# Carrying the last transposes of a sub-layer into the next one, in a two-layer hybrid decoder on eight cores

## What is computed

```python
for i in range(DEPTH):
    h = rms_norm(x, norm_g[i, 0])
    if i % N_MIXERS == 0:
        m, vr = spatial_gate_mixer(h, sg_w_in[j], sg_ln_g[j], sg_ln_b[j], sg_w_s[j], sg_b_s[j], sg_w_out[j])
    else:
        m, S = gla_mixer(h, gla_w_in[j], ..., gla_w_out[j], gla_init[j])
    x = x + rms_norm(m, norm_g[i, 1])
    h = rms_norm(x, norm_g[i, 2])
    x = x + rms_norm(swiglu(h, ffn_w13[i], ffn_w2[i]), norm_g[i, 3])
```

## Time and profile before

| | us |
|---|---|
| median of 2 runs | 2412.22 (2394.37 and 2430.08) |
| profiled execution | 2396.78 |
| its span, slowest core (6) | 2395.2 |
| spans of the eight cores | 2367.0 to 2395.2 |
| PE, DVE, ACT, POOL busy | 1819.7, 683.4, 693.8, 377.5 |
| TensorE's granted clock, mean of core 6 | 0.880 |

### The profile page before, as it was taken

One profiled execution on the slowest core, in us unless ns is written; L12 is line 12 of the kernel. 1 busy time (PEld: TensorE's weight loads), 2 busy tenths in 40 slices (PEclk: granted clock), 3 DMA queues, 4 the chain that ended last, 5 costly groups with the idle time before them and its releaser, 6 DMA issues.

```text
span 2395.2 us, 28534 instructions; the slowest of 8 cores (2367.0 to 2395.2 us)
## 1 busy us (share of the span) xinstructions
PE 1819.7 (76%) x9813; PEld 867.2 (36%) x9813; DVE 683.4 (29%) x1509; ACT 693.8 (29%) x1280; POOL 377.5 (16%) x447
## 2 busy tenths in 40 slices
PE   1698967697688966698587967599558898764698
PEld 0344423343344433343234433244224443321353
DVE  1422123312332122322233122322253212234222
ACT  2332134311422135411422125411423213542211
POOL 2011111311101111411111110411111111030010
PEclk9899988798799988699789988799779899875799
DMA  9789967289597959089696959189754882916572
GB/s 140 97 119 128 145 98 114 36 121 161 98 140 112 152 85 136 9 127 150 128 141 91 164 76 136 18 124 143 172 104 67 132 132 36 159 27 210 128 114 61
DMA packets 267997, 271.37 MB, mean 113 GB/s; under 512 B 17808, under 2 KB 261152, under 8 KB 267456
## 3 DMA queue, kind: packets, MB, share of 16 engines
q0 software_dynamic: 233088, 222.46, 64.6%
q1 hardware_dynamic: 26320, 38.71, 5.9%
q10 hardware_dynamic: 8448, 8.39, 1.1%
HBM read 473.44 MB, written 18.55 MB: 205 GB/s over the span
## 4 chain that ended last, share of the span: by engine, by line
PE 61%; DVE 11%; DMA 8%; ACT 7%; issue 7%; POOL 4%; SPq 1%; DVEq 0%; ACTq 0%; POOLq 0%
PE ps L244 57%; DMA yp<-t 4%; ACT t L313 2%; POOL t L303 2%; DVE t L602 2%; ACT t L331 1%; PE pt L348 1%; DMA t<-st_in 1%; DMA t<-sg_ln_b 1%; DVE t L369 1%; POOL t L942 1%; DVE t L372 1%; DVE t L388 1%; SPq L295 1%; DVE t L392 1%
## 5 line engine op out<-in xcount | busy, mean ns | idle before, releaser
L244 PE MATMUL ps<-t,t 128*128 128x512 bf16 (+4 forms) x8312 | 1656.6, 361 | 75.2 <-DVE t L923 25.4
L244 PEld LDWEIGHTS ps<-t,t 128*128 128x128 bf16 (+1 forms) x8312 | 750.7, 101 | 948.8 <-issue 217.2
L1054 DVE TENSOR_TENSOR t<-t,ps 128x512 bf16<-128x512 bf16 (+3 forms) x244 | 128.6, 541 | 510.5 <-PE ps L244 492.3
L348 PE MATMUL pt<-t,t 128*128 128x128 bf16 (+1 forms) x544 | 52.0, 255 | 286.6 <-ACT t L331 216.9
L262 POOL DMA_DIRECT2D t<-ffn_w x144 | 125.8, 876 | 895.9 <-PE ps L244 823.6
L1052 ACT ACTIVATE t<-ps 128x512 bf16<-128x512 f32 (+3 forms) x244 | 117.1, 480 | 502.5 <-PE ps L244 496.9
L303 POOL TENSOR_TENSOR t<-t,t 128x1 f32<-128x1 f32 (+1 forms) x136 | 74.8, 550 | 568.2 <-DVE t L301 568.2
L348 PEld LDWEIGHTS pt<-t,t 128*128 128x128 bf16 (+1 forms) x544 | 40.6, 115 | 306.6 <-issue 304.9
L313 ACT ACTIVATE t<-t 128x1024 bf16<-128x1024 f32 (+1 forms) x68 | 71.7, 1054 | 230.3 <-DVE t L372 103.2
L353 DVE TENSOR_TENSOR t<-pt,t 128x1024 bf16<-128x1024 bf16 (+1 forms) x68 | 79.0, 1169 | 141.9 <-PE pt L348 141.8
L301 DVE TENSOR_SCALAR t<-t 128x1 f32<-128x1 f32 (+1 forms) x136 | 20.5, 151 | 295.4 <-ACT t L313 165.4
(11 more groups left out here) (126 smaller groups left out, 1055.0 us busy)
## 6 DMA issues: line engine op xcount, KB each, us to landing
t<-ffn_w POOLq DMA_DIRECT2D x112, 1024.0 KB, 14.5
t<-sg_w_in POOLq DMA_DIRECT2D x32, 1024.0 KB, 20.1
t<-gla_w_in POOLq DMA_DIRECT2D x24, 1024.0 KB, 14.7
t<-sg_w_out POOLq DMA_DIRECT2D x16, 1024.0 KB, 19.9
t<-ffn_w POOLq DMA_DIRECT2D x16, 768.0 KB, 12.2
t<-xp SPq DMA_DIRECT2D x16, 512.0 KB, 5.1
t<-norm_g SPq DMA_DIRECT2D x16, 512.0 KB, 6.7
t<-ffn_w POOLq DMA_DIRECT2D x16, 512.0 KB, 9.5
```

The lines of the kernel that those rows point to most:

```text
L244: ins = e.matmul(out_ap, l, r, start=(i == 0), stop=(i == n - 1))
L348: ins = e.transpose(pt[:, pb, kc * 128: kc * 128 + np_], hbuf[0:np_, kc * 128:(kc + 1) * 128], ident[0:np_, 0:np_])
L1054: P.op(DVE, lambda e: e.tensor_tensor(out=gTf[:, j, t0:t1], in0=sab[sb][:, 0:n], in1=bank(ba + 1, 128, n), op=ALU.mult), reads=[("sab", sb ...
```

## The change

A list `carryB` holds `norm_in_B` calls that are put off, and `pop_carry` makes them: with a tile as argument the first one if it is that tile's, without one all of them. It is used at four places in passes 0 to 2:

- end of the gMLP mixer and end of the GLA mixer: `norm_in_B` of tile 3 is carried and made in the FFN behind its three units on tiles 0 to 2, ahead of the deferred units;
- end of FFN 0: the lag becomes 2, and `norm_in_B` of the last tile is carried and made in the V projection, ahead of tile 3's matmuls;
- end of FFN 1: `norm_in_A` of tiles 0 to 3 stays, and `norm_in_B` of all four is carried into the next mixer, each ahead of its tile's `vA`.

`hbx` gets addresses of its own at the end of SBUF, since it is now read while the mixer's tiles are in use.

```diff
+    HBX0 = (229344 - 4 * 2048) // 64 * 64
...
-    hbx = [alloc([128, D], BF16, a) for _ in range(4)]
+    assert a[0] <= HBX0
+    a_hbx = [HBX0]
+    hbx = [alloc([128, D], BF16, a_hbx) for _ in range(4)]
...
+    carryB = []
+
+    def pop_carry(tile=None):
+        while carryB and (tile is None or carryB[0][0] == tile):
+            norm_in_B(*carryB.pop(0))
+            if tile is not None:
+                break
...
                 for (t, np_) in tiles:
+                    pop_carry(t)
                     vA(t, np_)
...
-                norm_in_B(*pend)
+                if last:
+                    norm_in_B(*pend)
+                else:
+                    carryB.append(pend)
...
                         for (t, np_) in tiles:
+                            pop_carry(t)
                             b = bcx[0] % 4
...
-                        norm_in_B(te, 128, stt_[te]["hi"], li * 2 + 1)
+                        if (not last) and te == ptl[-1]:
+                            carryB.append((te, 128, stt_[te]["hi"], li * 2 + 1))
+                        else:
+                            norm_in_B(te, 128, stt_[te]["hi"], li * 2 + 1)
...
                     if jj == 0 and ci == NSPLIT - 1:
+                        pop_carry()
                         for d_ in deferred:
                             ab_unit(*d_)
...
-                lagn = (len(tiles) + 1) if final else 1
+                lagn = (len(tiles) + 1) if final else (2 if split else 1)
...
             while pendq:
-                norm_in_B(*pendq.pop(0))
+                if (not last) and len(pendq) == 1:
+                    carryB.append(pendq.pop(0))
+                else:
+                    norm_in_B(*pendq.pop(0))
             for (t, np_) in chained:
                 hi = norm_in_A(t, np_, xi=t)
-                pendq.append((t, np_, hi, 0))
-            while pendq:
-                norm_in_B(*pendq.pop(0))
+                carryB.append((t, np_, hi, 0))
```

More of the change, by code:

```diff
@@ L188, in _build @@
     mixs = alloc([16, 2048], BF16, a)
+    assert a[0] <= HBX0, (a[0], HBX0)
     a = phase_alloc()
```

## The result

| | before | after |
|---|---|---|
| median, us | 2398.09 (10 runs, 2391.72 to 2430.08) | 2463.78 (11 runs, 2441.08 to 2666.99) |
| ratio, 95% interval | | 1.0215 [1.0179, 1.0251] |
| profiled execution, us | 2396.78 | 2464.41 |
| span of the slowest core (6) | 2395.2 | 2462.8 |
| median span of cores 0 to 3 | 2378.8 | 2431.5 |

The ratio leaves out disturbed runs, in which the cores of one die showed a lower clock, and the medians don't; in the profiled execution after, too, cores 4 to 7 hold stretches of 66 to 162 us at a clock of 0.81 and cores 0 to 3 none, so what follows is read on core 0, or as a median over cores, unless it says core 6. 1.0215 on 2396.8 us is +51.5 us; the interval leaves no doubt that the kernel is slower, but it doesn't settle whether by more than 2%. A second series gave 1.022 [1.0168, 1.0272].

What follows compares the result with a forecast made beforehand. The prediction took TensorE's work plus its idle stretches, which also lower its clock, as the bound. Terms -9 (A), -22.5 (B), 0 (C) and +82.2 (D) sum to +50.7 on 2396.8 us: 2447, range 2428 to 2479.

Steps and rivals of the forecast that it cites:

- A: End of gMLP mixer to FFN 0: tile 3's transposes behind three units shorten TensorE's gap; -9 us over three passes.
- B: FFN 0 to GLA: lag of 2 and V projections ahead of tile 3's transposes; -22.5 us over three passes.
- C: GLA to FFN 1: 1.5 us gained at unit 0, 1.6 us waited in the deferred units; sum 0.
- D: FFN 1 to next pass's mixer: copies queue behind statistics on VectorE, TensorE idles; +82.2 us over three boundaries.
- The rival in which VectorE takes a ready copy first: At the pass boundary, ready copies pass the statistics, so deferral gains there: 2341 us, faster by 2.3%; chance 0.06.
- The holes: Idle TensorE ahead of `vA(1)`, `vA(2)` and `vA(3)` at each pass boundary: 7.6, 7.6 and 6.0, together 21.2 us.
- The earlier start: Next mixer's `vA(0)` starts at 613.6 instead of 615.41, at the low clock; worth 1.0 us a boundary.
- The low clock: Matmuls restarting after each of three pass-boundary gaps run at 0.50: 2.4 us a gap, 7.2 in all.
- The rows I named beforehand: Profile after: transposes' wait for ScalarE falls some 60 us; new matmul-for-copy row, nine waits of 6 to 8 us.
- Late slabs: Gains at FFN 0 and GLA don't arrive because weight slabs come late: 2479 us; chance 0.08.
- Bursts that never come back to the full clock: Pass boundary: each 32-matmul burst takes 13.8 us, never reaching full clock; +40, 2488 us; chance 0.05.
- A clock that doesn't fall: In the pass-boundary gaps the clock stays up: 20 us less, 2427 us; chance 0.05.

Runs made afterwards that it cites:

- the interleaved kernel: The changed kernel with norm_in_B of tiles 0 and 1 written between the norm_in_A, those of tiles 2 and 3 ahead of the statistics: 2353.59 us, 0.9807.
- the kernel without D: The changed kernel with the four norm_in_B at the pass boundary made ahead of the mixer again, everything else kept: 2370.14 us, 0.9878.

## Why the prediction was right

It gave 2447 us for a run like the profiled one, +50.7. The ratio gives +51.5; the measured median, 2463.78, lies in the range (2428 to 2479) 17 us above the figure. The narrower range of the forecast, 2434 to 2462, isn't the sum of its terms' bounds, which is 2427 to 2468; +51.5 lies inside either. By place, after against before in the stretches above:

| | predicted | measured |
|---|---|---|
| A | -9 | -6.9 |
| B | -22.5 | -22.6 |
| C | 0 | +0.3 |
| D | +82.2 | +74.6, and +2.9 up to the u projection |
| sum | +50.7 | +48.3 |

The remaining 3 us up to the ratio's 51.5 are in none of the four stretches; where they are is open. The mechanisms and the terms came out as forecast, to a few us; that the sum is within 1 us is luck, since D was put 4.7 us too high, A 2.1 us too good, and 3 us have no place.

**What TensorE waits for.** The step that decided the case was to ask, for the copy and not for the transposes, what stands in front of it on its engine. It held: the copy started as soon as L572 let it, and moving it ahead took 58 us back. The rival in which VectorE takes a ready copy first (2341 us) is refuted by the row at 615.69, 5.6 us after its transposes had ended. The Trainium skill states the rule that speaks here in TensorE: Matmul & The Clock Gate (Architectural detail), strict first in, first out for ScalarE and VectorE; this trace agrees for both, by that row and by the 6.07 us that a Gelu behind a waiting Square cost in the interleaved kernel.

**D, its terms.** The holes were put at 7.6, 7.6 and, beyond what stands there before, 6.0 us: 21.2. Core 0 shows 6.92 and 7.01 us of idle time, and from the end of one `vA` to the start of the next, with the transposes inside it, as the prediction counted, 617.05 - 609.68 = 7.4 and 633.80 - 626.34 = 7.5 us. From `vA(2)` to `vA(3)` it is 652.21 - 643.25 = 9.0 us, where the kernel before took 641.13 - 638.23 = 2.9: 6.1 more. Over cores and boundaries the medians, less what stood there before, are 7.5, 7.5 and 6.1: the delay, the heart of the matter, was right. The earlier start was put at a net 1.0 us a boundary; `vA(0)` starts 1.5 us earlier (89.4 to 84.9 in three) and ends 1.3 us earlier. The low clock was put at 2.4 us a hole, 7.2. The first two give 2.3 and 2.4 over the cores. The third gives 1.1: `vA(3)` takes 25.2 us in three, with 20.1 at the full clock, but before it already took 21.8, because its start was at the low clock at 6 of 18 boundaries then. That is 1.3 us a boundary too much, 4 of the 4.7 us between 82.2 and 77.5.

**A, its one bad term.** The place, the releaser (L374, before L369) and the gap under 4 us came as predicted, 3.79 us. The gain was 2.3 us a pass instead of 3.0. I had taken 4.75 us for the low stretch after the restart, the mean of 3.8 and 5.7. It lasted 6.8 us, 744.5 to 751.3. The matmuls filled 5.86 us of it and lost half of that, 2.9 us instead of 2.4, which is 0.5 of the 0.7 us that are missing. The same code gained from 6.9 to 11.3 us in the five kernels that have it, so the size is known no better than that.

**B and C.** B is met in its sum and in both parts, the lag 2.7 and the carry 4.5 against 2.6 and 4.9. The order is as worked out too: the copy of tile 2 starts 0.1 us after tile 3's L306, and tile 2's matmuls wait 1.25 us for it. One sentence isn't: the carry doesn't remove the low-clock stretch. It moves it to 874.2 to 884.4, where it makes 16 V matmuls take 5.76 us, and that costs nothing, since the next ones wait for the copy anyway. C's trade of a gap for a wait in the deferred units came out even, as said; the two gaps on core 0 after the change:

```profile
1012.06 10.64 PE L249 MATMUL ps<-t,t 128*128 128x384 bf16 x48 [2.44 <-DVE t L358]
...
1024.75 5.43 PE L249 MATMUL ps<-t,t 128*128 128x128 bf16 x60 [1.61 <-DVE t L358]
```

**The rows I named beforehand.** The wait of the transposes for ScalarE was to fall by some 60 us and fell by 84.1, and the new row was to hold some 60 and holds 139.4. The nine waits of 5.5 to 7 us are there, and they make 58. I left out 15 short ones at A, B and C, 28 us in the kernel without D, and what I forgot is that the first matmuls of `vA(0)` now wait for the first copy themselves. Those are three waits of up to 18.7 us. Before, part of that time was booked to the transposes, which waited there for the copy that frees their buffer, and the rest to their wait for ScalarE. From the list of waits of the kernel before:

```profile
PE pt L348 <- DVE t L353: 34.2, 3, 12.2
```

The row isn't in the list of after; the one at 613.58 in the earlier trace rows is one of its three. The waits moved to the new row and cost nothing new, since `vA(0)` starts sooner than before. A row's total changes with who stands in front, and it isn't a sum of cost; the time between two points that both kernels pass is.

**The other rivals.** Late slabs: FFN 0's and GLA's gains arrived in full in the kernel without D (0.9878), so no. Bursts that never come back to the full clock: 32 matmuls took 8.8 to 9.5 us, not 13.8. A clock that doesn't fall: refuted by the four stretches at 0.50.

## What to carry to other kernels

Before you move work to a later place to give an engine something to do, list for each engine that takes part what then stands between it and its input in program order; a 1.2-us copy queued behind a chain that waits for other engines costs the whole chain, here 7 us a tile, and moving it a few lines up makes the same deferral pay. Interleave in the order in which results become needed: copies ahead of the statistics, a Gelu that frees a bank ahead of a Square that still waits for its input. Judge such a change by place, between marks that both kernels pass, since here +77 us and -29 us were in one diff, and three of its four parts lost nothing.

## What the runs showed of the hardware that I had not expected

- The low clock lasts longer than the earlier trace rows led me to think. In the four stretches shown for the kernel after, at holes of 3.79 to 7.01 us, it stayed at 0.50 (1.2 of 2.4 GHz) for 6.8 or 6.9 us, and around the 8.52 us at the end of FFN 0 for 10.2 us, part of it still in the gap; how much is lost depends on how much of that the matmuls fill, here 1.7 to 2.5 us for 32 of them.
- A gap of 2.86 us was enough to bring it down where TensorE had been thinly busy ahead of it (the mixing matmuls of `vB`, in groups of four and eight between waits). It takes less: in the kernel before, with gaps of 1.17 and 0.65 us between those groups, core 0 falls to 0.50 for 3.4 us at the same place, at all three boundaries, and three other cores at one each. Gaps of 1.25 to 1.61 us in dense work never did in the rows shown above.

```profile
623.95 0.38 PE L596 MATMUL ps<-t,t 128*128 128x128 bf16 x4 [1.17 <-DVE t L602]
624.98 0.38 PE L596 MATMUL ps<-t,t 128*128 128x128 bf16 x4 [0.65 <-DVE t L602]
625.20 8.76 PE L244 MATMUL ps<-t,t 128*128 128x512 bf16 x32
...
625.80:629.20 3.40, 3.40 (x9) 1.22 (x8) 2.13 (x13) 0.69 (x2) 0.55 (x1) 0.50 0.00 0
```

- Useless matmuls in a gap can pay: 26 of them in each of two holes a boundary made the kernel after faster, 1.0168 against 1.022, though not as fast as closing the holes.
